# New prologue with a third piece of the modulation on TensorE, late constants, and the triangular inverse in 32x32 tiles, in a hybrid attention layer

## What is computed

```python
mod = silu(c) @ ada_w + ada_b                      # 1024 -> 3072
shift, scale, gate = split(mod, 3)
h = rmsnorm(x, pre_norm_w) * (1 + scale) + shift   # 256 x 1024
proj = h @ w_in                                    # 1024 -> 4104 columns
mq, mk, mv, mg, dq, dk, dv, dz, db, da = split(proj)
o_moba = causal_attention(rope(mq), rope(mk), mv) * silu(mg)    # 8 heads of 64, one block of 256
dq, dk, dv = split(silu(causal_conv4([dq, dk, dv])))            # 4 heads of 128
g, beta = -exp(a_log) * softplus(da + dt_bias), sigmoid(db)
# gated delta rule in 4 chunks of 64 tokens; per head and chunk:
A = (k * beta) @ k.T * decay_strict                # strictly lower triangular, 64 x 64
T = inverse(I + A)                                 # 64 x 64
u, w = T @ (v * beta), T @ (k * beta * exp(G))
# then chunk after chunk: v_new = u - w @ state; o = q @ state + qk @ v_new; state update
o_dn = rmsnorm(o, dn_norm_w) * silu(dz)
y = [o_moba, o_dn] @ w_out
out = x + gate * rmsnorm(y, post_norm_w)
```

## Time and profile before

| | us |
|---|---|
| median of the 3 runs | 191.32 |
| lowest and highest | 190.97, 197.76 |
| profiled execution | 190.73 |
| its span | 188.9 |
| TensorE busy in the span | 178.0 (94%) |
| VectorE, ACT, GpSimd busy | 141.5, 101.5, 77.5 |

### The profile page before, as it was taken

How to read it: one execution, slowest core, us unless ns; L and a number is a source line. 1 busy time by engine, 2 the same in 40 slices (tenths; PEclk the granted TensorE clock), 3 DMA queues, 4 the chain that set the end, 5 groups by cost and what they waited for, 6 DMA issues and landing times.

```text
span 188.9 us, 4380 instructions
## 1 busy us (share of the span) xinstructions
PE 178.0 (94%) x1718; PEld 161.5 (85%) x1718; DVE 141.5 (75%) x345; ACT 101.5 (54%) x195; POOL 77.5 (41%) x42
## 2 busy tenths in 40 slices
PE   7999989889999998999999999999999999999980
PEld 6769879789999998998998999999998987888850
DVE  0359699893459988998999787889689777858074
ACT  2645444439368878956562270455384448636230
POOL 2036627335687922985055068224913200810000
PEclk9999999999999999999999999999999999999998
DMA  5999999999519980300901807006942983020023
GB/s 160 403 386 394 393 409 407 407 397 404 218 16 367 395 328 8 114 0 2 323 14 17 319 8 212 13 0 220 362 201 78 344 356 119 14 97 0 3 111 111
DMA packets 12246, 38.41 MB, mean 203 GB/s; under 512 B 1473, under 2 KB 1857, under 8 KB 11714
## 3 DMA queue, kind: packets, MB, share of 16 engines
q1 hardware_dynamic: 12082, 37.61, 53.6%
q10 hardware_dynamic: 144, 0.52, 0.8%
HBM read 37.08 MB, written 1.05 MB: 202 GB/s over the span
## 4 chain that ended last, share of the span: by engine, by line
PE 69%; DVE 16%; DMA 6%; SPq 5%; issue 2%; ACT 1%; POOL 1%; DVEq 0%; POOLq 0%; ACTq 0%
PE bank L1395 16%; PE bank L1397 15%; PE bank L1396 15%; DVE cv L958 6%; DMA ada<-in_ada 6%; DVE bank L934 4%; SPq L351 3%; PE bank L1641 3%; PE bank L1630 3%; PE bank L1738 2%; PE bank L1745 2%; SPq L368 1%; PE bank L1754 1%; PE bank L1604 1%; PE bank L1666 1%
## 5 line engine op out<-in xcount | busy, mean ns | idle before, releaser
L474 POOL TENSOR_TENSOR wlo<-raw,whi 128x1024 fp32r<-128x1024 f32 (+1 forms) x25 | 58.1, 2334 | 62.2 <-ACT whi L543 62.2
L1395 PE MATMUL bank<-hhi,whi 128*128 128x256 f32 x218 | 63.1, 289 | 1.6 <-DVE hlo L906 1.1
L1396 PE MATMUL bank<-hhi,wlo 128*128 128x256 f32 x218 | 61.6, 283 | 0.0
L1397 PE MATMUL bank<-hlo,whi 128*128 128x256 f32 x218 | 61.6, 283 | 0.0
L1395 PEld LDWEIGHTS bank<-hhi,whi 128*128 128x128 f32 x218 | 41.7, 191 | 3.3 <-issue 1.8
L543 ACT ACTIVATE whi<-raw 128x1024 fp32r<-128x1024 f32 (+1 forms) x33 | 33.3, 1023 | 16.5 <-PE bank L1397 7.4
L1396 PEld LDWEIGHTS bank<-hhi,wlo 128*128 128x128 f32 x218 | 41.8, 192 | 0.0
L1397 PEld LDWEIGHTS bank<-hlo,whi 128*128 128x128 f32 x218 | 41.7, 191 | 0.0
L958 DVE SCALAR_TENSOR_TENSOR cv<-bank,convh,cv 128x255 f32<-128x255 f32 (+2 forms) x36 | 17.0, 481 | 5.6 <-ACT cv L609 4.6
L934 DVE SCALAR_TENSOR_TENSOR bank<-ada,sml,bank 128x256 f32<-128x256 f32 (+1 forms) x24 | 14.9, 621 | 0.7
L1157 DVE SCALAR_TENSOR_TENSOR accg<-ada,sml,accg 128x512 f32<-128x512 f32 x16 | 12.0, 751 | 2.7 <-DMA ada<-in_gate_w 2.3
(11 more groups left out here) (223 smaller groups left out, 337.6 us busy)
## 6 DMA issues: line engine op xcount, KB each, us to landing
raw<-in_w_rest SPq DMA_DIRECT2D x20, 512.0 KB, 4.8
ada<-in_ada SPq DMA_DIRECT2D x16, 256.0 KB, 7.1
ada<-in_ada SPq DMA_DIRECT2D x8, 512.0 KB, 12.0
ada<-in_gate_w SPq DMA_DIRECT2D x4, 1024.0 KB, 6.9
raw<-in_w_out SPq DMA_DIRECT2D x8, 512.0 KB, 5.7
raw<-in_w_qkv SPq DMA_DIRECT2D x5, 384.0 KB, 8.2
qkvs<-in_w_qkv SPq DMA_DIRECT2D x4, 384.0 KB, 11.2
cv<-in_w_qkv SPq DMA_DIRECT2D x4, 384.0 KB, 12.7
```

Of the source, the lines that this page charges most:

```text
L474: pool.tensor_tensor(split_u(wlo, n), raw_u(n), split_u(whi, n).bitcast(F32), ALU.subtract).then_inc(lo_done, 1)
L1395: pe.matmul(out, a[0][ia], b[0][ib], start=start, stop=False, skip_group_check=skip)
L1396: pe.matmul(out, a[1][ia], b[0][ib], start=False, stop=False, skip_group_check=skip)
L1397: return pe.matmul(out, a[0][ia], b[1][ib], start=False, stop=stop, skip_group_check=skip)
```

## The change

1. The product of piece 2 of the modulation moves from VectorE to TensorE (`ROWS = 3`). Its rows go to bank 6, those of pieces 0 and 1 stay in bank 7. `mod_rows(1)` and `mod_rows(2)` are interleaved in the order in which the halves of the transfers are to land, and `first_qkv_products` goes ahead of them, with its low-weight products last.
2. The row norm: the copy of the rows moves from ACT to VectorE, `x_sums` becomes one product with a 128x128 stationary of ones that gives the sums on all partitions for all 256 tokens, root and reciprocal work on 128x256, and `x_spread` goes away. One square of x moves from VectorE to ACT. Three filler products go away.
3. All constants but the first `NROWS` = 89 columns are loaded late in one transfer; `ba_turn` and `start_inverse` wait for it.
4. The inverse keeps 32-row blocks packed in `t32` (128x32 a head) up to level 4. A call of `z_products` or `x_products` has four 32x32 stationary tiles with 16 moving columns a head. `spread` builds the 64-wide T from the packed one, and the last level has calls of its own with two 32x32 tiles a head (`last_z_products`, `z_copy` on ACT, `last_x_products`, `last_merge`).
5. `DVE_LO` has 7 units rather than 12: VectorE makes the low parts of units 1, 10, 33 and 39 to 42, GpSimd all others. The order of transfers and of the steps of every engine is new.

```diff
-C_ID, C_IC, C_COS, C_SIN, C_TRI, C_CHK, C_MA, C_MQ, C_CM, C_LV = (NROWS + o for o in (0, 192, 256, 512, 768, 896, 1024, 1088, 1152, 1408))
-NCONST = C_LV + LEVELS * HALF
+C_ID, C_IC, C_COS, C_SIN, C_TRI, C_CHK, C_MA, C_MQ, C_CM, C_LV = (NROWS + o for o in (0, 192, 224, 480, 736, 864, 992, 1056, 1120, 1376))
+QUART = HALF // 2
+C_OWN = C_LV + HALF + (LEVELS - 2) * QUART
+NCONST = C_OWN + 2
...
-        ROWS = 2
+        ROWS = 3
...
-        DVE_LO = (5, 9, 11, 14, 21, 31, 35, 36, 40, 41, 42, 43)
+        DVE_LO = (1, 10, 33, 39, 40, 41, 42)
...
-                sp.dma_start(cst[:, 0:C_COS], const[:, 0:C_COS]).then_inc(front_loaded, 16)
+                sp.dma_start(cst[:, 0:NROWS], const[:, 0:NROWS]).then_inc(front_loaded, 16)
...
                 if p == 5 and g0 == 0:
-                    sp.wait_ge(acc_done, 2)
+                    sp.wait_ge(rows_made, 3)
+                    sp.wait_ge(acc_done, 1)
...
             load_unit(0)
+            load_ada(1, 2, 4)
+            load_ada(2, 0, 2)
             load_ada(1, 0, 2)
-            load_ada(1, 2, 4)
             load_unit(1)
-            load_ada(2, 0, 2)
+            load_ada(2, 2, 4)
             load_unit(2)
-            load_ada(2, 2, 4)
             load_unit(3)
+            load_ada(3, 0, 2)
             load_unit(4)
-            load_ada(3, 0, 2)
+            load_ada(3, 2, 4)
             load_unit(5)
-            load_ada(3, 2, 4)
+            load_ada(4, 0, 2)
             load_unit(6)
-            load_ada(4, 0, 2)
+            load_ada(4, 2, 4)
             load_unit(7)
-            load_ada(4, 2, 4)
             load_unit(8)
             load_ada(5, 0, 2)
+            load_unit(9)
+            load_gate_bias()
             load_unit(10)
-            load_unit(9)
             load_ada(5, 2, 4)
...
# GpSimd: start_inverse between lo(15) and lo(16), it stood behind lo(22)
-                pool.tensor_copy(tt[:, :, :], cst[:, C_IC:C_IC + CHUNK].unsqueeze(1).to_broadcast([P, NTH, CHUNK])).then_inc(tt_init, 1)
+                pool.tensor_copy(t32[:, :, :], cst[:, C_IC:C_IC + HALF].unsqueeze(1).to_broadcast([P, NTH, HALF])).then_inc(tt_init, 1)
...
# ACT
-                act.activation(sml[:, 18:20], bank[5][:, S:S + 2], ACT.Sqrt, scale=1.0 / D, bias=epsc[:, 0:1]).then_inc(xstd_done, 1)
+                act.activation(bank[5][:, S:], bank[5][:, S:], ACT.Sqrt, scale=1.0 / (32 * D), bias=epsc[:, 0:1]).then_inc(xstd_done, 1)
...
+            def z_copy(t):
+                act.wait_ge(z_ready, NT * (LEVELS - 2) + t + 1)
+                for c in range(2):
+                    q = quarter(2 * c)
+                    act.activation(heads(zt, t)[q], blocks(2 + 2 * t, 0, HALF)[q], ACT.Copy).then_inc(last_z, 1)
...
# VectorE
-                dve.reciprocal(sml[:, 20:22], sml[:, 18:20]).then_inc(xrstd_done, 1)
+                dve.reciprocal(bank[5][:, S:], bank[5][:, S:]).then_inc(rs_ready, 1)
...
-                    dve.transpose(heads(ti, t), heads(tt, t)).then_inc(ti_done, 1)
+                    dve.transpose(heads(ti32, t), heads(t32, t)).then_inc(ti_done, 1)
...
+            def spread(t):
+
+                dve.wait_ge(t_done, NT * (LEVELS - 2) + t + 1)
+                dve.tensor_tensor(heads(tt, t).rearrange("p h (a j) -> p h a j", a=2), heads(t32, t).unsqueeze(2).to_broadcast([P, DH, 2, HALF]),
+                                  cst[:, C_OWN:C_OWN + 2].unsqueeze(1).unsqueeze(3).to_broadcast([P, DH, 2, HALF]), ALU.mult)
+
+            def last_merge(t):
+                dve.wait_ge(x_ready, NT * (LEVELS - 2) + t + 1)
+                for c in range(2):
+                    q = quarter(2 * c)
+                    ins = dve.tensor_scalar(heads(tt, t)[q, :, HALF:], blocks(2 + 2 * t, 256, HALF)[q], -1.0, None, ALU.mult)
+                ins.then_inc(t_done, 1)
...
             conv(3)
+            conv_silu(0)
             gates_in()
+            conv_silu(1)
             rope(0)
-            conv_silu(0)
-            conv_silu(1)
             gates_out()
...
# TensorE
-                for t in range(NT):
-                    ins = pe.matmul(bank[5][:, S + t:S + t + 1], acc[:, 1, t * P:(t + 1) * P], epsc[:, 2:3], start=True, stop=True)
-                ins.then_inc(xsum_ready, 1)
+                pe.matmul(bank[5][:, S:], ones[:, :], acc[:, 1, 0:S], start=True, stop=True).then_inc(xsum_ready, 1)
...
-                    for c in range(2):
-                        r = rows_of(c)
-                        ins = pe.matmul(blocks(b, 0, HALF)[r, h, :], am[r, i, :], odd(tt[r, i, :], l), start=True, stop=True)
+                    for n in range(4):
+                        q, o = quarter(n), n % 2 * HALF
+                        ins = pe.matmul(blocks(b, 0, QUART)[q, h, :], am[q, i, o:o + HALF], odd(t32[q, i, :], l), start=True, stop=True)
...
+                    for n in range(4):
+                        q = quarter(n)
+                        ins = pe.matmul(blocks(2 + 2 * t, 256, QUART)[q, h, :], ti32[q, i, :], zt[q, i, 0:QUART], start=True, stop=True)
+                ins.then_inc(x_ready, 1)
+
+            def last_z_products(t):
...
             mod(0)
-            x_spread()
             busy(1, 2)
+            first_qkv_products()
+            mod_rows(1, 3)
             mod_rows(1, 0)
...
-            first_qkv_products()
+            mod_rows(2, 4)
+            mod_rows(2, 2)
+            mod_rows(2, 6)
+            mod_rows(2, 3)
+            mod_rows(2, 7)
             mod(1)
+            mod(2)
             qkv_products(1)
-            mod(2)
...
+            qkv_products(10)
             mod(5)
-            qkv_products(10)
...
+            k_turn(0)
             cum()
-            k_turn(0)
...
-            v_turn(1)
             z_products(3, 0)
             z_products(3, 1)
-            p_turn(1)
             x_products(3, 0)
             x_products(3, 1)
+            v_turn(1)
+            p_turn(1)
             z_products(4, 0)
             z_products(4, 1)
             x_products(4, 0)
+            x_products(4, 1)
+            half(11)
+            last_z_products(0)
+            last_z_products(1)
             pv(1)
-            x_products(4, 1)
-            z_products(5, 0)
-            z_products(5, 1)
-            x_products(5, 0)
-            x_products(5, 1)
+            last_x_products(0)
+            last_x_products(1)
+            half(12)
             w_products(0)
             w_products(1)
             u_products(0)
-            half(11)
-            half(12)
```

360 lines of the change are left out of this document (190 added, 170 removed).

## The result

| | before | after |
|---|---|---|
| median of the runs, us | 191.18 | 201.07 |
| lowest and highest | 190.97, 197.76 | 198.26, 202.64 |
| profiled execution, its span | 190.73, 188.9 | 201.75, 199.7 |
| mean granted clock of that execution | 0.996 | 0.954 |

The ratio is 1.043, with a 95% interval of 1.030 to 1.057, which is 8.2 us. The forecast was 187.3 us, with a range up to 192.5. Most kernels of this study now and then take some 3 to 7 us more in an execution, and the ratios leave those executions out, while the medians have them in: of the changed kernel 201.75 us (the profiled one) and 202.64 us. The two that count took 198.26 and 200.40 us at mean clocks of 0.965 and 0.963, where the kernel before has 0.99 to 1.00.

What follows compares the result with a forecast made beforehand. TensorE, busy 178.0 of 188.9 us, was taken as the bound. Prologue -2.0, gap -0.35 and inverse -1.7 summed to -4.05 us, from a median of 191.3 to 187.3 us; range 185.4 to 192.5 us.

Steps and rivals of the forecast that it cites:

- the first paragraph: What bounds the kernel: TensorE busy 178.0 of 188.9 us, clock 1.00 in every stage to 183.3 us, none to win.
- the pitch: Inverse: time per instruction on 32x32 tiles, taken as 13 ns; 576 instructions give 7.5 us of TensorE, term -1.7 us.
- The 25 ns: Inverse: least start-to-start distance by the skill's rule; 14.4 us for 576 instructions, +3.9 us, kernel about 192.9 us.
- The rest of the order: Moved halves, y_products and low parts: no TensorE work changed, costed at 0; behind 117 us order can only lose.
- a late half: Rest of the order: if a half starts late, it costs the wait, up to 2.4 us.
- The gap of 0.8 us: TensorE's wait before the cumulative sums, filled by the first turn of the keys: -0.35 us, between 0 and -0.83.
- The prologue: Stage to 38.44 us: piece 2 on TensorE and earlier sums end it sooner, -2.0 us, between 0 and -3.25.
- prologue hidden: Rival, 15%: TensorE waits for a weight unit behind an ada half; prologue term becomes 0, 189.3 us.
- the reciprocal: Prologue, row norm: root and reciprocal on 256 columns, bounds 0.17 and 0.42 us each, the upper taken.
- the end of the stage: Prologue: the stage of the qkv products was to end near 54.1 us instead of 56.1 us.
- The pitch of 22.7 ns: Inverse, in the 10% rival of 32.7 ns and 197.3 us: pitch at which the change becomes a loss.
- The forecast's own range: The 45% case, 187.3 us: from all prologue idle time won to half the prologue term lost.

Runs made afterwards that it cites:

- e2: The kernel before with only the new 32x32 inverse, all other orders as there: 199.85 us, ratio 1.043.
- e5: e2 with half of the 32x32 tiles left out in levels 1 to 4, output not the reference's: 195.85 us, ratio 1.015.
- e13: The kernel before with only TensorE's order around the inverse as in the changed kernel, 64x64 tiles kept: 201.34 us, ratio 1.053.
- e14: e13 with 24 useless products (48 instructions, 11.5 us) put behind levels 1 to 4 of the inverse: 209.56 us, ratio 1.097.
- e15: e2 with 24 useless products (48 instructions, 11.5 us) put behind levels 1 to 4 of the inverse: 201.4 us, ratio 1.052.
- e19: e15 with a third of its useless products (16 matmuls, 3.8 us): 205.47 us, ratio 1.074.
- e16: e1 with four GpSimd low parts made to wait for VectorE's sums and other steps: 194.70 us, ratio 1.020.
- e3: The changed kernel with weight units from 33 on issued only after level 3 of the inverse: 201.19 us.
- e8: The kernel before with the changed kernel's order on all queues from the end of the inverse on, low-part shares included: 193.14 us, ratio 1.008.
- e1: The changed kernel with the old 64x64 inverse back, all orders as changed: 196.15 us, ratio 1.025.
- e12: The kernel before with only k_turn(0) moved ahead of cum(): 193.07 us, ratio 1.011.
- e10: The kernel before with the changed prologue, late constants and order up to the last qkv product: 190.92 us profiled; 197.45, 197.72 and 198.15 otherwise.
- e4: The changed kernel with four more filler products ahead of the first products of h: 200.32 us, ratio 1.046.
- e11: e10 with the norm's reciprocal replaced by a copy of the same size, output not the reference's: 198.32 us, ratio 1.038.

## Why the prediction was wrong

**The clock.** The step that failed is in the first paragraph: the granted clock is 1.00 in every stage, so no clock is to be won. I went on as if none could be lost, and put no term for it into the sum. In the profiles of the new inverse alone (e2), of half of its tiles (e5) and of the new order alone (e13) the clock is 0.50 to 0.51 from 110 to 123 us; fillers between the levels hold it, or nearly (1.00 in e14, 0.91 in e15), though a third of them does not (e19). The kernel before kept its clock with the 64x64 tiles and with `v_turn(1)`, `p_turn(1)`, `pv(1)` between the levels. Changing either one lost it, the order not in every execution (e16). I priced a tile by the time between two starts only. TensorE: Matmul & The Clock Gate, Part 1, of the Trainium skill, says that half rate is the default and that activity releases the full one. The rows have these two levels, and the lower one came here while the profile had TensorE busy for 16.9 of 18 us (e13). How many of the 8.2 us are the clock, no run shows by itself: what e14 and e15 got back is mixed with idle time and a shorter stop.

**The inverse: the pitch was right and the sign wrong.** I took 13 ns from the earlier trace rows, and it is 12.7 ns (64 from 106.41 to 107.22 us), at 2.4 GHz. The 25 ns of the Trainium skill (TensorE: Matmul & The Clock Gate, Part 1) did not come true. Its warning on a dimension that is already small (TensorEngine Tiling (Array Packing), Instruction Overhead) pointed the right way for another reason than a cost of each product. What was missing is the supply of instructions. At 13 ns a matmul with its load, 201 matmuls go out in 2.65 us, and then TensorE stops: for 2.61 and 1.35 us (2.99 in e2), gone when the count is halved (e5). That they go out faster than they are brought is what this and the packets of e3 point to. The forecast was -1.7 us, e2 shows +8.2. Of this 3 us are the stop itself, and the rest is put down to the clock. e5, without the stop, is at +2.8 with less work in it, so the split is rough.

**The rest of the order.** I wrote that no order behind 117 us can win anything, it can only lose, and then priced it at 0, with "up to 2.4 us" for a late half. e8 has 1.6 us, and in the changed kernel the late part has 3.5 us of waits for VectorE. The mechanism behind these waits was not the one I named. GpSimd's low part does not have to be late; it is enough that it is running when VectorE begins an operation on two operands from SBUF (`kT`, `accg`, `olo`, `wlo`), for that operation then takes up to 2.2 us more, while those that read PSUM keep their length (`gm` 0.68 us inside a low part in the kernel before). With the low parts moved, the wait of 1.8 us for `stg` in e1 is gone (e16). SBUF — State Buffer, Who interferes with whom, of the Trainium skill states this rule, two SBUF inputs against a GpSimd instruction that reads SBUF, whoever starts first goes through; the trace agrees in every case above, and the prediction left it out, for a change that gives GpSimd more of them. Where the two start within 0.04 us of each other, the profile's starts do not tell who is held: in the changed kernel an `accg` sum stands at 137.81 us and GpSimd's low part at 137.85 us, and the sum takes 3.0 us.

**The gap of 0.8 us.** The step was right in itself: the wait fell from 0.82 to 0.34 us in the changed kernel, and to 0.38 us in e12. But e12 is 2 us slower. VectorE's low part began 0.2 us earlier and GpSimd's 0.9 us earlier, which turned their order round and set off one hold-up of 2.2 us.

**The prologue.** I said -2.0, bounded by 0, and e10 is at 0 in its one execution without the longer time: as far as that goes, my rival "prologue hidden" held here. And in the changed kernel the clock fell to 0.57 for 3.5 us of the prologue, a term that I did not have (1.2 us at the start of the inverse, e4). Mis-sized were the reciprocal (1.77 us for 256 columns, where I bounded it by 0.42 from an ordinary operation of that size) and, of more weight, the end of the stage. e11 starts 1.2 us earlier and arrives 0.25 us earlier. The DMA share of 1.03 in the earlier trace rows had pointed to it: I took the pieces of the modulation for the limit, and it was more likely the sum of all bytes, which no run made smaller.

**What the changed kernel's loss is made of.** It is 8.2 us by the ratios and 9.9 us by the medians. Undoing the inverse gives 3.5 to 4.9 us back (e1), moving the low parts 1.0 to 1.5 more (e16). The prologue is near 0 (e10). Some 3.5 us are left between e16 and the kernel before; the order around the inverse (clock 0.95 and 1.5 us idle from 106 to 124 us in e16) and the late order of e8 stand there, and no run divides them. The parts do not add up: the inverse alone costs the kernel before 8.2 us (e2), and the order around it by itself 10 us (e13).

**Sums of the prediction.** The pitch of 22.7 ns, at which the change was to turn into a loss, was worked out from 10.7 us for the old inverse rather than its 10.5, and would be 22.3 ns. The forecast's own range, from the terms as given, is 186.0 to 188.3 us rather than 185.4 to 188.6. Neither changes a reading.

## What to carry to other kernels

Where a stage of small tiles runs at the full clock, put a term for losing it into the sum before you make the tiles smaller or move the large products out from between them; a row of busy time does not show how safe the clock is. A burst of matmuls at 13 ns each can end in a stop that no wait in the kernel's text will show. And list, for each GpSimd instruction that reads SBUF, what VectorE begins during it: in a kernel with no slack on TensorE, a shift of under 1 us between the two cost 2 us (e12).
